# Modulation matrix multiplied as plain float32 on four 32-column tiles, with straight-line programs

## The chip, the cores and the metric

One core of one Trainium2 chip. The metric is device time of the whole kernel in microseconds; the kernel before takes 3344.34 us (median of three runs). PE is the engine for matrix products (TensorE), DVE VectorE, ACT ScalarE, POOL GpSimd, SP SyncE; SP and POOL only issue transfers here.

## What is computed

One inference step of a two-layer backbone on 128 context and 128 latent tokens of width 2048, all in float32. Layer 0 mixes tokens by attention, layer 1 by a two-directional state-space scan; each is followed by an MLP of width 8192. Every sub-layer is modulated, from a linear map of a conditioning vector:

```python
def ada_mod(cond, w, b):
    m = jax.nn.silu(cond) @ w + b          # w: 2048 x 12288 for each layer
    return jnp.split(m[:, None, :], 6, axis=-1)

for i in range(DEPTH):                     # 2 layers
    mp = ada_mod(c_ctx[None, :], mod_w[i], mod_b[i])   # context tokens
    ms = ada_mod(c, mod_w[i], mod_b[i])                # latent tokens
    hp = modulate(rms_norm(xp, norm_mix[i]), mp[0], mp[1])   # h * (1 + scale) + shift
    ...                                    # attention or scan
    xp = xp + mp[2] * op
    hp = modulate(rms_norm(xp, norm_mlp[i]), mp[3], mp[4])
    xp = xp + mp[5] * (jnp.square(jax.nn.relu(hp @ mlp_w1[i])) @ mlp_w2[i])
    ...                                    # the same for xs with ms
```

So the modulation matrices (two of 2048 x 12288, 201 MB) meet only two vectors, silu(c_ctx) and silu(c), while the other weights (some 450 MB) meet 256 tokens.

## The kernel before

All weights stream through SBUF in chunks of 1 MB (512 x 512 float32, as four blocks of 128 rows side by side, 2 KB pieces). A chunk lands in one of four slots of `raw`, in the order that SP issues. Each chunk is **split**: ACT writes `w_hi`, the rounding of `raw` to the reduced float32r type (two halves of 128 x 1024), and DVE writes `w_lo` = `raw` - `w_hi` (`split`, lines 441 and 697; two buffers of each). A slot is free again when DVE has read it (`lo_ready`).

An **L chunk** is one of a weight matrix. PE multiplies 16 blocks of 128 x 128: `hi` with 512 columns (256 tokens, high and low part; line 1111) and `lo` with the 256 high columns (lines 1110 and 1113), into four PSUM banks. Four L chunks (2,048 rows) make a **group** of 512 outputs; then ACT evacuates the right half of each bank (line 490), DVE adds the left half (line 787) and does the group's own work (`finish`).

An **M chunk** is one of the modulation matrix, split in the same way. PE holds as weights a window of `cond_w` (four columns carry silu of both vectors, high and low, the rest is other blocks' columns or zeros) and streams 512 columns of `w_hi` and then `w_lo` for each of four row blocks: eight products (line 1094) into bank `MROW`. After four M chunks ACT copies four rows of `MROW` to `m_rows` (line 478), four small float32 products with `comb` turn them into columns in `MCOL` (line 1141), and DVE adds the bias into `modv` (line 767): 48 times in all.

`layout` lists the phases. A phase has a pattern: "M" (eight groups of M chunks first, the shift and scale of layer 0), "LM" (an M chunk ahead of each L chunk: q, k, v, wo, the four `up0` and z) and "L" (the rest). There are 192 M and 432 whole L chunks. On each engine the middle groups of a phase are a hardware loop (`runs`, `Fori`), the first and last are written out.

Each engine's program is in order. At the end of a group ACT and DVE split the next chunk first (`nxt`) and evacuate then; in an LM phase that next chunk is an M chunk, so the first L chunk of the next group is split after the evacuation. Norms (`norm`) run between phases: ACT squares, 16 float32 products with ones on PE (line 1158), root, reciprocal, and then per quarter of the rows scaling on DVE and the high and low operand; some splits stand between these steps by `first_splits`. The scan of layer 1 is straight-line code; there, products on two 64-column tiles of the array alternate (`unit`, line 1318), beside products on the whole array (lines 1328 and 1347).

Of the kernel before, what the change touches and what calls it, by code (L numbers as in the profile page):

```python
# [25 lines left out]
ALU = mybir.AluOpType  # L26
# [22 lines left out]
HALF = CH_KT // 2 * CH_N  # L49
RAW_SLOTS = 4  # L50
MOD_BLOCKS = 6 * KT
N_QUARTERS = DFF // D

PAT = {
    "M": [("M", q) for q in range(4)],
    "L": [("L", q) for q in range(4)],
    "LM": [(t, q) for q in range(4) for t in ("M", "L")],
}


class Phase:


    def __init__(self, name, kind, pat, n, w=None, k0=0, c0=0, mod=None, operand=None, width=CH_N, **more):
        self.name, self.kind, self.pat, self.n = name, kind, pat, n
        self.w, self.k0, self.c0, self.mod, self.operand, self.width = w, k0, c0, mod, operand, width
        self.more = more
        self.chunks = PAT[pat]
        self.m = len(self.chunks)


def layout(ins):

    (mod_w, w1, w2, wqkv, wo, w_in, w_out) = (ins[k] for k in (
        "mod_w", "mlp_w1", "mlp_w2", "na_wqkv", "na_wo", "ssm_w_in", "ssm_w_out"))
    ph = [Phase("mod", "mod", "M", 8, mod=(0, 0))]
    for j, kind in enumerate("qkv"):
        ph.append(Phase(kind, kind, "LM", 4, w=wqkv[0], c0=j * D, mod=(0, 8 + 4 * j), operand="HL"))
    ph.append(Phase("wo", "res", "LM", 4, w=wo[0], mod=(0, 20), operand="HID", layer=0, gate=2 * KT))
    for layer in range(2):  # L80
        if layer == 1:
            ph.append(Phase("dt", "dt", "L", 1, w=w_in[0], c0=D_INNER + XBC_TILES * P, operand="HL", width=P))
            ph.append(Phase("z", "z", "LM", 8, w=w_in[0], c0=0, mod=(1, 16), operand="HL"))
            ph.append(Phase("xbc", "xbc", "L", 12, w=w_in[0], c0=D_INNER, operand="HL"))
            for half in range(2):
                ph.append(Phase(f"wout{half}", "res", "L", 4, w=w_out[0], k0=half * KT,
                                operand=("HL", "HID")[half], layer=1, gate=2 * KT))
        for quarter in range(N_QUARTERS):
            ph.append(Phase(f"up{layer}_{quarter}", "w1", "L" if layer else "LM", 4, w=w1[layer], c0=quarter * D,
                            mod=None if layer else (1, 4 * quarter), operand="HL"))  # L90
            ph.append(Phase(f"down{layer}_{quarter}", "res", "L", 4, w=w2[layer], k0=quarter * KT,
                            operand="HID", layer=layer, gate=5 * KT))
    t = g = mg = 0
    for p in ph:
        p.T0, p.G0, p.M0 = t, g, mg
        t += p.m * p.n
        g += p.n if "L" in p.pat else 0
        mg += p.n if "M" in p.pat else 0
    return ph


def chunk_source(ins, p, col0, typ, q):

    if typ == "M":
        layer, g0 = p.mod
        view = ins["mod_w"][layer].rearrange("(t p) n -> p t n", p=P)
        return view[:, 4 * q:4 * q + 4, bass.ds(g0 * CH_N + col0, CH_N)]
    view = p.w.rearrange("(t p) n -> p t n", p=P)
    return view[:, p.k0 + 4 * q:p.k0 + 4 * q + 4, bass.ds(p.c0 + col0, p.width)]


def program(nc, ins, outs):
    ph = layout(ins)
    by_name = {p.name: p for p in ph}
    N_CHUNKS = ph[-1].T0 + ph[-1].m * ph[-1].n
    owner = [p for p in ph for _ in range(p.m * p.n)]

    def by_block(p, c):


        typ, q = p.chunks[c]
        return typ == "L" and (q == 3 or (q == 0 and p.pat == "L") or p.width < CH_N)

    def read_count(T, u):

        p = owner[T]
        return 4 * T + 4 if by_block(p, (T - p.T0) % p.m) else 4 * T + 2 * (u + 1)

    ctx = ExitStack()
    with ctx:  # L130
# [48 lines left out]
        comb = sb("comb", [4, 2])  # L179
# [6 lines left out]
        csil = sb("csil", [P, 2, KT], offset=at_R + 40960)  # L186
# [37 lines left out]
        w_read = sem("w_read")  # L224
        evac = sem("evac")
        bank_free = sem("bank_free")
        group_out = sem("group_out")
        e2_step = sem("e2_step")
# [36 lines left out]
        G_END = {p.name: p.G0 + p.n for p in ph if "L" in p.pat}  # L265
        block = ctx.enter_context(nc.Block())

        def runs(eng, p, body):

            if p.n <= 2:  # L270
                for i in range(p.n):
                    body(i, 0)
                return
            body(0, 0)
            if p.n == 3:
                body(1, 0)
            else:
                with eng.Fori(0, p.n - 2) as s:
                    body(1, s)
            body(p.n - 1, 0)  # L280

        def first_splits(p):


            if p.pat == "LM":
                return {0: ((), (2,)), 1: ((), (3, 4)), 2: ((), (5, 6)), 3: ((), (7,))}
            return {0: ((), ()), 1: ((), ()), 2: ((2,), ()), 3: ((3,), ())}

        after_norm = {1, 5, 13, 16, 18}


        @block.sync
        def _(sp):
# [28 lines left out]
            for p in ph:  # L322
# [1100 lines left out]
```

## Time and profile before

| | |
|---|---|
| timed runs | 3344.34 us median, 3342.19 to 3346.95 |
| profiled execution, span first to last instruction | 3336.6 us |
| median of the runs above that span | 7.7 us |
| PE, DVE, ACT busy | 94%, 66%, 52% of the span |
| transfers | 696.17 MB, 209 GB/s mean over the span |

The profiled execution is one execution; the page gives its span, and its own time is that span with what lies around it, for which the only figure is the distance to the timed runs. In the rows, `bank<-HL,w_hi` means that the instruction writes `bank` and reads `HL` and `w_hi`; L1111 is a line of the kernel; `x192` counts records. A float32 product leaves two weight-load and two matmul records (a high and a low half), a float32r product one of each. PEclk is the granted TensorE clock as a share of full speed. Records of PE overlap in its pipeline.

### The profile page before, as it was taken

What the parts mean: (1) busy time and instruction counts of PE and PEld (TensorE: products, weight loads), DVE (VectorE), ACT (ScalarE), POOL (GpSimd) and SP (SyncE); (2) the same over time, 40 slices, a digit from 0 to 9 for tenths busy, and PEclk for the clock granted to TensorE, in tenths of its full rate; (3) what the DMA queues carried; (4) which work ended last, traced back from release to release, by engine and by line L of the source; (5) the groups of instructions that cost most, each with busy time, mean ns of one, the idle gap of its engine ahead of it and who ended that gap; (6) DMA issues with size and microseconds to landing.
All of it is one profiled execution on the core that took longest, in us unless ns stands there. A gap on an engine that the chain in (4) does not pass through costs nothing.

```text
span 3336.6 us, 47767 instructions
## 1 busy us (share of the span) xinstructions
PE 3119.8 (94%) x17357; PEld 2663.5 (80%) x17357; DVE 2215.8 (66%) x2980; ACT 1723.2 (52%) x2247; POOL 44.2 (1%) x71
## 2 busy tenths in 40 slices
PE   6899998989999999999699999966698999999998
PEld 4688887878888888888588888856587888888887
DVE  7866666777666676675666566777766665666565
ACT  5655555555455454454466555567443444444443
POOL 1000000000000000000000000011000000000000
PEclk9999999999999999999899999977899999999999
DMA  9777774757567576674477655556254555555552
GB/s 321 267 273 262 272 274 151 263 197 271 189 239 252 182 271 214 218 273 151 162 253 252 241 176 189 188 171 192 81 188 151 169 184 189 189 179 186 190 188 88
DMA packets 378477, 696.17 MB, mean 209 GB/s; under 512 B 12192, under 2 KB 55392, under 8 KB 377360
## 3 DMA queue, kind: packets, MB, share of 16 engines
q1 hardware_dynamic: 373568, 676.38, 59.3%
q0 software_dynamic: 4816, 18.69, 1.6%
q8 instruction: 42, 0.69, 0.1%
q14 instruction: 51, 0.42, 0.0%
HBM read 686.50 MB, written 8.52 MB: 208 GB/s over the span
## 4 chain that ended last, share of the span: by engine, by line
PE 39%; DVE 7%; issue 2%; ACT 2%; DMA 1%; SPq 1%; DVEq 0%; ACTq 0%; POOL 0%; POOLq 0%
PE bank L1111 24%; PE bank L1110 12%; PE bank L1094 1%; DMA bc_prompt<-ac_scratch 1%; DVE w_lo L697 1%; ACT w_hi L441 1%; PE bank L1113 1%; SPq L311 1%; DVE bc_prompt L992 0%; PE bank L1359 0%; DVE ROOM L746 0%; DVE xd L958 0%; DVE ROOM L751 0%; DVE ROOM L757 0%; DVE bc_prompt L948 0%
## 5 line engine op out<-in xcount | busy, mean ns | idle before, releaser
L697 DVE TENSOR_TENSOR w_lo<-raw,w_hi 128x1024 fp32r<-128x1024 f32 x1256 | 1481.1, 1217 | 731.3 <-ACT w_hi L441 730.9
L441 ACT ACTIVATE w_hi<-raw 128x1024 fp32r<-128x1024 f32 x1256 | 1268.0, 1050 | 1028.3 <-PE bank L1111 999.2
L1111 PE MATMUL bank<-HL,w_hi 128*128 128x512 f32 x4368 | 1549.7, 401 | 68.8 <-DVE HL L815 28.6
L1110 PE MATMUL bank<-HL,w_lo 128*128 128x256 f32 x4095 | 1162.8, 284 | 27.6 <-DVE HL L815 13.7
L1111 PEld LDWEIGHTS bank<-HL,w_hi 128*128 128x128 f32 x4368 | 814.4, 190 | 252.4 <-issue 61.3
L1111 PE MATMUL bank<-HID,w_hi 128*128 128x512 f32 x2560 | 894.2, 398 | 0.3 <-DVE w_lo L697 0.3
L1110 PEld LDWEIGHTS bank<-HL,w_lo 128*128 128x128 f32 x4095 | 781.1, 191 | 63.8 <-DVE w_lo L697 28.9
L1110 PE MATMUL bank<-HID,w_lo 128*128 128x256 f32 x2400 | 674.8, 281 | 0.0
L1111 PEld LDWEIGHTS bank<-HID,w_hi 128*128 128x128 f32 x2560 | 471.1, 188 | 105.1 <-issue 1.5
L1110 PEld LDWEIGHTS bank<-HID,w_lo 128*128 128x128 f32 x2400 | 453.6, 189 | 7.7 <-DVE w_lo L697 0.7
L787 DVE TENSOR_TENSOR U<-bank,U 128x256 f32<-128x256 f32 x433 | 181.1, 422 | 257.5 <-ACT U L490 257.4
L490 ACT ACTIVATE U<-bank 128x256 f32<-128x256 f32 x433 | 164.0, 383 | 339.6 <-PE bank L1111 336.4
L1094 PE MATMUL bank<-w_hi,cond_w 128*128 128x512 f32 x768 | 312.9, 407 | 8.3 <-DVE w_lo L697 7.3
L1094 PE MATMUL bank<-w_lo,cond_w 128*128 128x512 f32 x768 | 305.2, 397 | 0.0
L1094 PEld LDWEIGHTS bank<-w_hi,cond_w 128*128 128x128 f32 x768 | 146.1, 190 | 45.0 <-DVE w_lo L697 16.8
L1094 PEld LDWEIGHTS bank<-w_lo,cond_w 128*128 128x128 f32 x768 | 146.0, 190 | 31.2
L738 DVE SCALAR_TENSOR_TENSOR X<-U,modv,X 128x128 f32<-128x128 f32 (+1 forms) x352 | 96.1, 345 | 0.4
L1113 PE MATMUL bank<-HL,w_lo 128*128 128x256 f32 x273 | 79.2, 290 | 0.0
L1113 PEld LDWEIGHTS bank<-HL,w_lo 128*128 128x128 f32 x273 | 55.0, 202 | 11.4
L1141 PEld LDWEIGHTS bank<-comb,m_rows 4*128 4x128 f32 x384 | 46.2, 186 | 19.3 <-issue 9.9
L515 ACT ACTIVATE HL<-SQ 128x1024 fp32r<-128x1024 f32 x16 | 16.9, 1058 | 81.7 <-DVE SQ L833 81.7
L1141 PE MATMUL bank<-comb,m_rows 4*128 4x2 f32 x384 | 50.3, 249 | 5.9 <-ACT m_rows L478 5.9
(203 smaller groups left out, 1377.0 us busy)
## 6 DMA issues: line engine op xcount, KB each, us to landing
raw<-in_mlp_w SPq DMA_DIRECT2D x256, 1024.0 KB, 5.2
raw<-in_mod_w SPq DMA_DIRECT2D x192, 1024.0 KB, 6.0
raw<-in_ssm_w_in SPq DMA_DIRECT2D x80, 1024.0 KB, 5.0
raw<-in_na_wqkv SPq DMA_DIRECT2D x48, 1024.0 KB, 5.1
raw<-in_ssm_w_out SPq DMA_DIRECT2D x32, 1024.0 KB, 5.0
raw<-in_na_wo SPq DMA_DIRECT2D x16, 1024.0 KB, 5.0
bc_prompt<-ac_scratch SPq DMA_DIRECT2D x16, 512.0 KB, 5.7
bc_sample<-ac_scratch SPq DMA_DIRECT2D x16, 512.0 KB, 6.0
```

The lines of the kernel that those rows point to most:

```text
L311: sp.dma_start(ea[64 * h:64 * h + 64, d, :, :], src).then_inc(ea_in, 16)
L441: nc.scalar.activation(w_hi[:, T % 2, u * n:(u + 1) * n], raw[:, T % RAW_SLOTS, u * n:(u + 1) * n], ACT.Copy).then_inc(hi_ready, 1)
L490: i = nc.scalar.activation(U[:, b, :], bank[b][:, TOK:2 * TOK], ACT.Copy)
L515: nc.scalar.activation(HL[:, 4 * t:4 * t + 4, 0:TOK], SQ[:, 4 * t:4 * t + 4, :], ACT.Copy).then_inc(oper_hi, 1)
L697: nc.vector.tensor_tensor(w_lo[:, T % 2, s], raw[:, T % RAW_SLOTS, s], w_hi[:, T % 2, s], ALU.subtract).then_inc(lo_ready, 1)
L738: i = nc.vector.scalar_tensor_tensor(xt, U[:, b, r * SEQ:(r + 1) * SEQ], gt, xt, ALU.mult, ALU.add)
L787: i = nc.vector.tensor_tensor(U[:, b, :], bank[b][:, 0:TOK], U[:, b, :], ALU.add)
L1094: i = nc.tensor.matmul(MROW[:, :], lhs, w[:, slot, kt * CH_N:(kt + 1) * CH_N], start=first, stop=last)
L1110: nc.tensor.matmul(bank[b][:, 0:TOK], lo, a[:, 0:TOK], start=False, stop=False)
L1111: i = nc.tensor.matmul(bank[b][:, :], hi, a, start=first, stop=last)
L1113: i = nc.tensor.matmul(bank[b][:, 0:TOK], lo, a[:, 0:TOK], start=False, stop=False)
L1141: i = nc.tensor.matmul(MCOL[:, 2 * b:2 * b + 2], m_rows[:, b * P:(b + 1) * P], comb[:, :], start=True, stop=True)
```

## The change

The M chunk becomes 128 rows of 2,048 columns (8 KB pieces), read by PE directly from `raw` as plain float32. The weights are 32 columns (`cond`: silu of the two vectors and 30 zeros), and four products per chunk go to four 32-column tiles of the array, so that tile j writes partitions 32j to 32j + 31 of `MROW`. A block of 2,048 outputs takes 16 M chunks; then ACT copies all of `MROW` once, four products with `pick` turn it, and DVE adds the bias for 16 tiles of 128: 12 times in all. M chunks are no longer split; their slot is freed by PE (`m_read`). The load order is a list: 32 M chunks first, then one ahead of each L chunk of the former LM phases. All loops are written out. All groups now follow the order of the former L phases: the next L chunk's split stands ahead of the evacuation, and the by-block order of products holds at the first and last chunk of each group. The first norm moves into the first M stage. Core of the diff:

```diff
+def load_order(ph):
+    order = [("M", m) for m in range(MOD_FIRST)]
+    m = MOD_FIRST
+    for p in ph:
+        for i in range(4 * p.n):
+            if p.mod:
+                order.append(("M", m))
+                m += 1
+            order.append(("L", p.T0 + i))
+    return order
...
+def mod_source(ins, m):
+    layer, block, kt = m // (6 * KT), m // KT % 6, m % KT
+    return ins["mod_w"][layer][kt * P:(kt + 1) * P, block * D:(block + 1) * D]
...
-        cond_w = sb("cond_w", [P, KT * 4 + P - 4], F32R)
-        cond = cond_w[:, 0:KT * 4].rearrange("p (t v) -> p t v", v=4)
+        cond = sb("cond", [P, KT, 32])
-        m_rows = sb("m_rows", [4, CH_N])
+        m_rows = sb("m_rows", [P, CH_N])
...
# SP
+            for at, (typ, n) in enumerate(order):
+                if at >= RAW_SLOTS:
+                    gone, g = order[at - RAW_SLOTS]
+                    if gone == "L":
+                        sp.wait_ge(lo_ready, 2 * (g + 1))
+                    else:
+                        sp.wait_ge(m_read, g + 1)
...
# ACT
+            def mod_rows(block):
+                act.wait_ge(m_read, KT * (block + 1))
+                if block:
+                    act.wait_ge(m_cols, block)
+                nc.scalar.activation(m_rows[:, :], MROW[:, :], ACT.Copy).then_inc(m_rows_in, 1)
...
+                    if T + 4 < N_CHUNKS:
+                        split(T + 4)
+                    block = block_done(T)
+                    if block is not None:
+                        mod_rows(block)
...
+            squares(range(4))
+            norm_root()
+            for block in range(2):
+                mod_rows(block)
+            split(0)
+            split(1)
+            operand(by_name["q"])
...
# DVE, first norm
+                if k == 0:
+                    dve.wait_ge(rms_root, 1)
+                    link(nc.vector.reciprocal(rbc[:, :], rbc[:, :]))
+                    mod_bias(0)
+                    mod_bias(1)
+                    split(0)
                 if not last:
...
+                    split(p.T0 + 1)
...
# PE
-                                    for part, w in enumerate((w_hi, w_lo)):
-                                        i = nc.tensor.matmul(MROW[:, :], lhs, w[:, slot, kt * CH_N:(kt + 1) * CH_N],
-                                                             start=first, stop=last)
+            def mod_chunk(m):
+                block, kt = m // KT, m % KT
+                slot, full = loaded("M", m)
+                pe.wait_ge(raw_in[slot], full)
+                if kt == 0 and block:
+                    pe.wait_ge(m_rows_in, block)
+                for j in range(4):
+                    i = nc.tensor.matmul(MROW[32 * j:32 * j + 32, :], cond[:, kt, :],
+                                         raw[:, slot, j * CH_N:(j + 1) * CH_N], start=kt == 0, stop=kt == KT - 1)
+                i.then_inc(m_read, 1)
+            def mod_cols(block):
+                pe.wait_ge(m_rows_in, block + 1)
+                if block:
+                    pe.wait_ge(mod_out, block)
+                for b in range(4):
+                    i = nc.tensor.matmul(MCOL[:, 8 * b:8 * b + 8], m_rows[:, b * P:(b + 1) * P], pick[:, :],
+                                         start=True, stop=True)
+                i.then_inc(m_cols, 1)
...
+            for m in range(MOD_FIRST):
+                mod_chunk(m)
+                if m == KT // 2:
+                    norm()
+                if m % KT == KT - 1:
+                    mod_cols(m // KT)
```

In a phase, PE calls `mod_chunk` ahead of the L chunk that it stands before in the list, and `mod_cols` after the first L chunk of the group that follows a finished block.

## Rows read from the trace of the kernel before

**Rows 1.** The page: busy times; costly groups (count, busy us, mean ns, idle); a transfer.

```profile
PE 3119.8 (94%) x17357; PEld 2663.5 (80%) x17357; DVE 2215.8 (66%) x2980; ACT 1723.2 (52%) x2247; POOL 44.2 (1%) x71
...
L697 DVE TENSOR_TENSOR w_lo<-raw,w_hi 128x1024 fp32r<-128x1024 f32 x1256 | 1481.1, 1217 | 731.3 <-ACT w_hi L441 730.9
L441 ACT ACTIVATE w_hi<-raw 128x1024 fp32r<-128x1024 f32 x1256 | 1268.0, 1050 | 1028.3 <-PE bank L1111 999.2
...
raw<-in_mod_w SPq DMA_DIRECT2D x192, 1024.0 KB, 6.0
```

**Rows 2.** Windows: M and L chunks; L alone; first M stage (busy, clock, DMA).

```profile
391.59:484.98 93.39, 93.39 (x505) 79.38 (x505) 62.76 (x65) 53.71 (x64) 0.00 (x0) 1.00 0.76 270
2765.59:2856.00 90.41, 90.41 (x514) 78.56 (x513) 55.95 (x65) 38.86 (x48) 0.00 (x0) 1.00 0.56 186
39.00:106.00 67.00, 60.25 (x254) 42.33 (x253) 58.65 (x56) 53.10 (x57) 0.00 (x0) 0.99 1.04 383
```

**Rows 3.** Windows of line 1111 alone: stretch, us, PE, PEld, clock, DMA share, GB/s.

```profile
391.59:484.98 93.39, 67.37 (x192) 35.47 (x193) 1.00 0.76 270
2765.59:2856.00 90.41, 89.28 (x258) 47.05 (x256) 1.00 0.56 186
134.68:173.49 38.81, 24.08 (x64) 12.72 (x65) 0.94 0.54 190
...
707.26:1589.69 882.43, 722.07 (x2048) 379.40 (x2048) 0.99 0.65 224
2576.87:2607.51 30.64, 25.84 (x65) 13.90 (x65) 0.84 0.31 103
1636.37:1892.81 256.44, 181.55 (x512) 95.12 (x512) 0.99 0.74 258
1898.10:2173.44 275.34, 268.53 (x768) 141.49 (x768) 1.00 0.53 180
```

**Rows 4.** The chain that ended last, in z: start, us, what.

```profile
1709.34 1.86 PE bank L1094 x8
```

**Rows 5.** Timelines of PE, wide and narrow windows: start, us, engine, line, records.

```profile
690.75 1.05 PE L1141 MATMUL bank<-comb,m_rows 4*128 4x2 f32 x8
691.73 7.17 PE L1158 MATMUL bank<-SQ,one 128*128 128x256 f32 x32
...
2216.68 1.95 PE L1347 MATMUL bank<-ROOM,h0T 128*128 128x128 f32 x16
2218.56 1.97 PE L1318 MATMUL bank<-bc_sample,xd 128*64 128x128 f32 x32
...
2218.36 0.28 PE L1347 MATMUL bank<-ROOM,h0T 128*128 128x128 f32 x1
2218.56 0.33 PE L1318 MATMUL bank<-bc_sample,xd 128*64 128x128 f32 x2
...
2218.56 0.44 PE L1318 MATMUL bank<-bc_sample,xd 128*64 128x128 f32 x4
...
2327.66 0.28 PE L1318 MATMUL bank<-bc_prompt,xd 128*64 128x128 f32 x2
2327.86 0.38 PE L1328 MATMUL bank<-rbc,xd 128*128 128x128 f32 x1
```

**Rows 6.** Timeline at the end of down0_0 and before z.

```profile
930.58 3.89 ACT L441 ACTIVATE w_hi<-raw 128x1024 fp32r<-128x1024 f32 x4
...
934.63 0.79 PE L1111 MATMUL bank<-HL,w_hi 128*128 128x512 f32 x1 [2.53 <-DVE w_lo L697]
...
1636.37 0.79 PE L1111 MATMUL bank<-HL,w_hi 128*128 128x512 f32 x1 [7.39 <-DVE w_lo L697]
```

**Rows 7.** DMA queues from 2196 to 2330 us: packets, MB, share of 16 engines.

```profile
q8 instruction: 6, 0.10, 0.3%
```

**Rows 8.** Timeline of the start, PE.

```profile
26.91 0.48 PE L1094 MATMUL bank<-w_hi,cond_w 128*128 128x512 f32 x1
...
134.68 0.79 PE L1111 MATMUL bank<-HL,w_hi 128*128 128x512 f32 x1 [5.51 <-DVE HL L815]
```

More of the change, by code:

```diff
@@ L48 @@
 CH_N = 512
-HALF = CH_KT // 2 * CH_N
 RAW_SLOTS = 4
 MOD_BLOCKS = 6 * KT
+MOD_CHUNKS = 12 * KT
+MOD_FIRST = 2 * KT
 N_QUARTERS = DFF // D
[L54 to L58, printed above, removed]
-class Phase:
[L64 to L69, printed above, removed]
@@ L114, in program, with loaded, mods_before, block_done @@
     by_name = {p.name: p for p in ph}
[L115 to L122, printed above, removed]
+    N_CHUNKS = ph[-1].T0 + 4 * ph[-1].n
+    owner = [p for p in ph for _ in range(4 * p.n)]
+    order = load_order(ph)
+    place_of = {what: at for at, what in enumerate(order)}
+    def loaded(typ, n):
+        at = place_of[typ, n]
+        return at % RAW_SLOTS, 16 * (at // RAW_SLOTS + 1)
+    def mods_before(T):
+        at = place_of["L", T]
+        start = place_of["L", T - 1] + 1 if T else MOD_FIRST
+        return [n for _, n in order[start:at]]
+    def block_done(T):
+        for t in range(T // 4 * 4, T // 4 * 4 + 4):
+            for m in mods_before(t):
+                if m % KT == KT - 1:
+                    return m // KT
+        return None
+    def by_block(T):
+        return T % 4 in (0, 3) or owner[T].width < CH_N
     def read_count(T, u):
-        p = owner[T]
-        return 4 * T + 4 if by_block(p, (T - p.T0) % p.m) else 4 * T + 2 * (u + 1)
+        return 4 * T + 4 if by_block(T) else 4 * T + 2 * (u + 1)
     ctx = ExitStack()
@@ L263, in program, with first_splits @@
         f_sc, f_t, f_sb, f_done = (sem(n) for n in ("f_sc", "f_t", "f_sb", "f_done"))
-        G_END = {p.name: p.G0 + p.n for p in ph if "L" in p.pat}
+        G_END = {p.name: p.G0 + p.n for p in ph}
         block = ctx.enter_context(nc.Block())
[L268 to L289, printed above, removed]
+        def first_splits(t):
+            return {2: (2,), 3: (3,)}.get(t, ())
+        after_norm = {"q", "up0_0", "dt", "wout0", "up1_0"}
         @block.sync
@@ L459, in silu @@
                     nc.scalar.activation(v, v, ACT.Silu).then_inc(silu_out, 1)
-                def body(rep, shift):
+                for rep in range(p.n):
                     last = rep == p.n - 1
-                    for c in range(1, p.m):
-                        if rep or k not in after_norm:
-                            split(p.T0 + rep * p.m + c, p.m, shift)
+                    gi, T = p.G0 + rep, p.T0 + 4 * rep
+                    if rep or name not in after_norm:
+                        for c in (1, 2, 3):
+                            split(T + c)
@@ L713, in finish, with phase @@
+            def phase(name):
+                p = by_name[name]
+                def finish(rep):
+                    dve.wait_ge(bank_free, 4 * (p.G0 + rep + 2))
+                    tiles = slice(4 * rep, 4 * rep + 4)
                     Uall = U[:, :, :]
-                    def step(i, s):
-                        i.then_inc(e2_step, 1)
-                        dve.wait_ge(e2_step, e2_0 + steps * rep + s + steps * shift)
                     if p.kind in "qkv":
@@ L796, in _, with norm @@
             norms = [0]
-            def norm(layer, scale, shift_, gain, p=None, last=False):
+            def norm(layer, scale, shift_, gain, p=None, blocks=0, last=False):
                 k = norms[0]
                 norms[0] += 1
+                if k == 0:
[4 more added lines that the diff above has]
+                    split(0)
                 if not last:
-                    dve.wait_ge(mod_out, 1 + max(p.M0 + p.n for p in ph if "M" in p.pat and p.T0 < cur[0]))
+                    dve.wait_ge(mod_out, blocks)
@@ L939, in _ @@
             dve.wait_ge(ac_w, 16)
-            phase(15)
+            phase("xbc")
             def segments(g):
@@ L1402, in constants @@
     c[:, 4] = np.where(ok[turned], 0.0, NEG)
-    c[[0, 1, 2, 3], 5, [0, 1, 0, 1]] = 1.0
+    for j in range(4):
+        c[[32 * j, 32 * j + 1], 5, [2 * j, 2 * j + 1]] = 1.0
     return c
```

513 lines of the change are left out of this document (211 added, 302 removed).

## The prediction

> **What bounds the kernel now.** I read the page first. TensorE (PE) is busy 94% of the span, VectorE 66%, ScalarE 52% [rows 1]. PE's records overlap in its pipeline, so their sums are no prices; starts and stretches are. Then the stages: in a stretch where a modulation ("M") chunk goes before every weight ("L") chunk, and in one with L chunks alone, PE is busy the whole time, DVE 67% and 62%, ACT 58% and 43%, the DMA engines 0.76 and 0.56 [rows 2]. So PE sets the pace of both. In the first M stage (39 to 106 us) the DMA engines are full at 383 GB/s, with PE at 90%: DMA sets that one.
>
> Next the pace, by line 1111 (16 records per L chunk, 64 per group of four). L alone: 90.41 us for four groups, 22.60 each. With M: 93.39 us for three groups, 31.13 each [rows 3]. The difference, 8.53 us, is four M chunks and one small transposing product: the latter's eight records take 1.05 us [rows 5], an M chunk (line 1094, eight records) 1.86 us [rows 4], and 4 x 1.87 + 1.05 = 8.53. So 1.87 us per M chunk is PE's real price.
>
> **The change, part by part.**
>
> *The new M chunk on PE.* It holds 128 rows by 2,048 columns, as many numbers as before: four float32 matmuls of 512 columns, each a high and a low record. Plain float32 is in the trace: 32 records of 256 columns take 7.17 us [rows 5], about 0.216 us a record, so a 512-column record is 0.433 us. Eight in turn would be 3.46 us, nearly twice today's 1.87. All depends on whether the column tiles run at once. The trace shows no four tiles of 32 columns, but two of 64, also in float32, in the scan. There 32 records of 128 columns take 1.97 us; on the whole array 16 records take 1.95 us [rows 5]: 0.055 against 0.11 us a record. The narrow windows say how: the records come in pairs, from the first on; one on the whole array lasts 0.28 us, the first two here together 0.33 and the first four 0.44, so each pair starts together, 0.11 after the pair before. So two tiles do run side by side, each with its own high and low half in turn. If four do the same, the chunk is two steps of 0.433 = 0.87 us.
>
> Bounds: 0.87 us below; 3.46 us above (in turn); and 4 x 0.433 = 1.73 us if no more than the two streams that the trace shows are fed at once. I take 0.87, because the pairs show tiles as independent and nothing in the rows as a limit of two.
>
> *Changing the tile shape.* From whole array to 64 columns the next start comes 0.20 us after the last instead of 0.11, and the first record is 0.33 us long, not 0.28; going back it is 0.20 instead of 0.11, and 0.38, not 0.28 [rows 5]. That is 0.14 + 0.19 = 0.33 us a visit; each M chunk between L chunks is a visit. So 0.87 + 0.33 = 1.20 us, 0.67 less than now; bounds 0.87 (changes hidden) to 3.8.
>
> A rule speaks against the four at once. The pairs above start with the very first records. The Trainium skill (TensorE: Matmul & The Clock Gate, Part 3, "What overlaps and what doesn't") says that matmuls start and end strictly in order, and that a weight load overlaps a running matmul only in another row group, while column tiles share all rows. By that a tile's low half waits for its high half, and the next tile queues behind it: five steps. The trace disagrees for two tiles; no run here shows four. The rule's time is a rival below.
>
> *Transposing product.* Once per 16 chunks instead of four: 0.26 us a group instead of 1.05. A group with M is then 22.60 + 4 x 1.20 + 0.26 = 27.66 us.
>
> *ACT and DVE.* 384 splits of 1.05 and 1.22 us [rows 1] leave. Neither sets the pace, so by itself this is worth nothing; it pays where an L chunk's split stood late. At the end of an L phase that an M phase follows, ACT splits the next L chunk only after the last evacuation (930.58), DVE after its residual operations, and PE waits 2.53 us for it (934.63) [rows 6]. Now the split of the next L chunk stands ahead of the evacuation, as in L phases, where groups keep 22.6 us. The same order holds at every group of z.
>
> *Transfers.* A pair of chunks (2.1 MB) in 27.66 / 4 = 6.9 us is 304 GB/s; 383 has been granted [rows 2], so it is hidden. If only today's 270 came, the pair would take 7.8 us and all the gain of these stages would be lost. An M slot is now freed by PE, and SP's next L load queues behind that wait. With M done 1.2 us into a pair, the M load takes 6.0 us [rows 1] and the L load behind it 2.7 more: landed at 9.9, first half split at 12.2 (1.05 + 1.22). PE wants it at 13.8 + 1.2 = 15.0, so 2.8 us spare.
>
> *Straight-line programs.* A loop's return costs PE nothing now: in L phases 64 pairs of 0.353 us make the whole 22.60. So no gain there. More instructions must be fetched. In the scan, straight-line already, 6 packets came on PE's instruction queue in 134 us [rows 7], one per 22 us. I take zero, because PE's products in that stage run on at 0.11 and 0.055 us a record [rows 5]; exposed, a packet is about 1.1 us (0.3% of 16 engines' 134 us, over 6).
>
> *The start.* PE's first M chunk stands at 26.9 us, behind the transposes of x, and the first L product at 134.7 [rows 8]. Between 27 and 39 us slots still wait for M splits behind bias work on DVE; now PE frees them directly. From about 29 us DMA is full: 32 more chunks (M4 to M33, L0, L1; DVE splits L1 ahead of the first scaling) at 1.05 MB / 383 GB/s = 2.74 us, plus 3.3 us of latency (6.0 - 2.7), end at 120. Split of L1 3.3 (two halves on ACT, one more on DVE), then scaling, shift, copy and low half, an estimate of 5.7 (five passes of 128 x 1024 at 1.05 to 1.22): first L product at 129 us, now 134.7, so 6 us. The norm's 7.2 us on PE moves under the loads; the wait for L1 eats most of that. Bounds: nothing, or 22 us if the loads come faster.
>
> *Sum* [rows 3, 6]:
> - start: 6
> - q to wo: 15 groups x (31.13 - 27.66) = 52; the first, 38.81, becomes about 31, like the first group after a norm without M (30.64): 8
> - layer 0's MLP, 882.43 us: 31 + 15 x 27.66 + 16 x 22.60 = 807.5, and 1 from M0 under the norm: 76
> - z, 256.44 us: 8 x 27.66 = 221.3: 35. After dt, PE waits 7.39 us for z's first L split, held behind ACT's dt work; that split now comes first and its 5.65 us of products and an M chunk fill the wait: 7
> - xbc, 275.34 us against 12 x 22.60 = 271.2: 4, less 1 for the last transposing product: 3
>
> Together 187 us: 3336.6 - 187 = 3149.6 of span. The shown median is 7.7 us above the profiled span; I keep that: **3157 us**.
>
> **Rivals.**
> 1. *Four tiles at once* (forecast): 3157. For it the pairs; against it that only two are seen.
> 2. *Two streams at a time*: 1.73 + 0.33 = 2.06 us a chunk, 0.86 x 160 = 138 us back: 3295. For it: two float32 streams (512 columns in 0.433 us each) take columns about as fast as today's float32r stream (512 in 1.86 / 8 = 0.233), and no row shows more.
> 3. *In turn*, slower than before: if a tile's low half waits for its high half and the next tile's records queue behind it in order, five steps of 0.433 + 0.33 = 2.50 us a chunk give 208 back, 3365; wholly in turn 3.8 us, 416 back, and the 28 first chunks PE-bound at 3.8 instead of 2.74 (30 us): about 3603. It decides from 1.20 + 187 / 160 = 2.37 us a chunk. Against it the pairs in rows 5. The skill's order rule, above, is the five steps.
> 4. *Fetches exposed*: one packet per 22 us as in the scan, 143 x 1.1 = 157 us: 3314. Against it: the even pace of the scan's products.
> 5. *More gain*: shape changes hidden behind the last L product (160 x 0.33 = 53) and a quicker start (15): about 3090.
>
> **How the numbers follow.** Chances: 0.55 for the first, 0.20 for the second, 0.11 for the third, 0.06 for the fourth, 0.08 for the fifth. The time is the first's, 3157; its own range is 3120 to 3190 (0.1 us of shape change is 16 us, the start 15). For 8 in 10 the range reaches from the near half of the fifth to the second: 3105 to 3303. Faster by over 0.2% (what a measurement of this kernel can tell from no change): the first, second, fifth and half of the fourth, 0.86; same, the other half of the fourth (packets dearer still), 0.03; slower, the third, 0.11.
>
> **What would show it.** In the changed profile: records of the M products on 32 columns starting in fours 0.43 us apart, an M chunk about 1.2 us from the L product before to the one after; groups with M at 27.7 us and without at 22.6; near 300 GB/s in those stages with PE still busy throughout; transposing products 12 times, not 48; no ACT splits of M; no PE wait at L-to-M phase changes; first L product near 129 us. Steps of twos (1.7 us a chunk) mean rival 2, single ones rival 3. Wrong otherwise, if PE waits for raw data in the M stages, or waits of no cause come at even distances of instructions (fetches).

## The result and the profile after

The changed kernel takes 3134.91 us (median of four runs, 3133.77 to 3138.26) where the kernel before took 3344.78 in the same comparison: a ratio of 0.9379, interval 0.9365 to 0.9392. The forecast was 3157 (3105 to 3303), so the time lies 22 us below it and inside the range. The profiled span is 3133.4 us against 3336.6.

The page of the changed kernel, busy times and groups as in [rows 1]:

```profile
PE 2921.3 (93%) x17069; PEld 2371.7 (76%) x17069; DVE 1763.6 (56%) x2559; ACT 1279.7 (41%) x1796; POOL 44.0 (1%) x71
...
q8 instruction: 135, 2.21, 0.3%
...
L694 DVE TENSOR_TENSOR w_lo<-raw,w_hi 128x1024 fp32r<-128x1024 f32 x872 | 1033.9, 1216 | 941.7 <-ACT w_hi L439 941.7
L439 ACT ACTIVATE w_hi<-raw 128x1024 fp32r<-128x1024 f32 x872 | 884.6, 1049 | 1221.5 <-PE bank L1089 614.7
...
L1055 PE MATMUL bank<-raw,cond 128*32 128x512 f32 x1536 | 217.8, 644 | 25.6 <-DMA raw<-in_mod_w 25.6
```

L1055 is the new M product, L1089, L1091 and L1088 are the L products, L694 and L439 the splits on DVE and ACT. The 384 splits of M on each of these engines are gone (1256 to 872), and that takes 447 us of work from DVE and 383 from ACT; PE, whose records overlap, gives up 198. PE stays busy for 93% of the shorter span.

The stages, as windows of all engines (columns as in [rows 2]): three groups with M, four of L alone, the first M stage, z, xbc, layer 0's MLP.

```profile
264.95:346.19 81.24, 81.24 (x485) 60.52 (x481) 34.60 (x41) 28.69 (x37) 0.00 (x0) 1.00 0.85 306
2562.43:2652.84 90.41, 90.41 (x514) 78.52 (x513) 56.01 (x65) 38.75 (x48) 0.00 (x0) 1.00 0.60 188
39.00:106.00 67.00, 46.77 (x236) 12.98 (x240) 1.95 (x2) 1.07 (x2) 0.00 (x0) 0.70 0.94 387
...
1474.20:1691.47 217.27, 216.98 (x1285) 162.84 (x1282) 95.31 (x111) 87.11 (x111) 0.00 (x0) 1.00 0.85 307
1696.42:1968.16 271.74, 271.74 (x1547) 236.22 (x1545) 184.06 (x278) 129.58 (x158) 0.55 (x1) 1.00 0.54 183
635.97:1435.22 799.25, 798.27 (x4641) 642.28 (x4642) 444.56 (x584) 308.69 (x391) 0.00 (x0) 1.00 0.71 248
```

Against [rows 3], L alone has not moved: 90.41 us for four groups then and now. Three groups with M went from 93.39 to 81.24, so one is 27.08 us. An M chunk is then (27.08 - 22.60) / 4 = 1.12 us where it was 1.87; it was forecast at 1.20. PE is still busy without a gap in these stages, and DMA carries 306 GB/s there (forecast 304), so the transfers stayed hidden. The first M stage is still set by DMA (387 GB/s); PE is busy there for 47 of 67 us only.

One M chunk between two L chunks in PE's timeline, then the same chunk in narrow windows (start, us, engine, line, records):

```profile
433.72 0.39 PE L1089 MATMUL bank<-HL,w_hi 128*128 128x512 f32 x1
434.04 1.07 PE L1055 MATMUL bank<-raw,cond 128*32 128x512 f32 x8
435.04 0.39 PE L1088 MATMUL bank<-HL,w_lo 128*128 128x256 f32 x1
435.26 0.40 PE L1089 MATMUL bank<-HL,w_hi 128*128 128x512 f32 x1
...
434.04 0.62 PE L1055 MATMUL bank<-raw,cond 128*32 128x512 f32 x2
...
434.04 0.64 PE L1055 MATMUL bank<-raw,cond 128*32 128x512 f32 x4
...
434.49 0.61 PE L1055 MATMUL bank<-raw,cond 128*32 128x512 f32 x4
...
434.04 0.16 PEld L1055 LDWEIGHTS bank<-raw,cond 128*32 128x32 f32 x8 [0.25 <-issue]
```

The first two records together last 0.62 us and the first four 0.64: four products on four tiles start within about 20 ns. The second four start at 434.49, 0.45 us behind the first. So a chunk is two steps of 0.45 us, as the forecast had it (0.433). The five steps that were worked out for the third rival from the order rule in the Trainium skill (TensorE: Matmul & The Clock Gate, Part 3, "What overlaps and what doesn't") do not happen: no tile's high half waits for another's low half. The weight loads do not keep to that rule either, by which one overlaps a running product only in another row group: all eight of the chunk are over at 434.20 us, while its first products, on the same 128 rows, run until 434.66. The same part of that page, under "Measured speedup vs the span model", gives a measured speedup of 2.38 times for three column tiles; here four tiles make an M chunk 3.35 / 1.12 = 3.0 times as fast as the whole array does (first experiment, changes of shape included), which is in line with it.

The start, with the releaser in brackets:

```profile
116.23 2.00 ACT L439 ACTIVATE w_hi<-raw 128x1024 fp32r<-128x1024 f32 x2 [3.21 <-DMA raw<-in_na_wqkv]
117.39 2.36 DVE L694 TENSOR_TENSOR w_lo<-raw,w_hi 128x1024 fp32r<-128x1024 f32 x2 [2.82 <-ACT w_hi L439]
119.67 2.18 DVE L818 SCALAR_TENSOR_TENSOR SQ<-X,modA,rbc 128x128 f32<-128x128 f32 x8
...
125.52 0.80 PE L1089 MATMUL bank<-HL,w_hi 128*128 128x512 f32 x1 [13.28 <-DVE HL L805]
```

L1 lands at 116.2, its split on DVE ends at 119.7, and the first quarter of the operand follows: the first L product stands at 125.5 where it stood at 134.7 [rows 8]; the forecast was 129, with L1 landed at 120.

### The profile page after: what moved, and what is told of

The parts are those of the page before. It is cut to its first block, busy times and chain, and to the rows that moved or that the text cites. A ratio compares the mean times of both kernels' runs of the same rounds, so it can differ in the third digit from the quotient of the medians.

```text
span 3133.4 us, 40784 instructions
## 1 busy us (share of the span) xinstructions
PE 2921.3 (93%) x17069; PEld 2371.7 (76%) x17069; DVE 1763.6 (56%) x2559; ACT 1279.7 (41%) x1796; POOL 44.0 (1%) x71
## 4 chain that ended last, share of the span: by engine, by line
PE 44%; DVE 5%; DMA 1%; ACT 1%; issue 1%; SPq 1%; POOL 0%; DVEq 0%; ACTq 0%; POOLq 0%
PE bank L1089 28%; PE bank L1088 13%; DMA bc_prompt<-ac_scratch 1%; PE bank L1055 1%; PE bank L1091 1%; SPq L313 1%; PE bank L1327 1%; DVE w_lo L694 0%; DVE bc_prompt L969 0%; DVE xd L935 0%; DVE ROOM L1028 0%; DVE bc_prompt L925 0%; DVE ROOM L1026 0%; DVE SQ L818 0%; DVE ROOM L944 0%
## 5 line engine op out<-in xcount | busy, mean ns | idle before, releaser
L1089 PE MATMUL bank<-HL,w_hi 128*128 128x512 f32 x4368 | 1542.2, 399 | 56.2 <-DVE HL L805 38.0
L694 DVE TENSOR_TENSOR w_lo<-raw,w_hi 128x1024 fp32r<-128x1024 f32 x872 | 1033.9, 1216 | 941.7 <-ACT w_hi L439 941.7
L439 ACT ACTIVATE w_hi<-raw 128x1024 fp32r<-128x1024 f32 x872 | 884.6, 1049 | 1221.5 <-PE bank L1089 614.7
L1088 PE MATMUL bank<-HL,w_lo 128*128 128x256 f32 x4095 | 1167.7, 285 | 18.6 <-DVE HL L805 16.9
L1089 PEld LDWEIGHTS bank<-HL,w_hi 128*128 128x128 f32 x4368 | 811.7, 189 | 256.9 <-DVE HL L805 41.5
L1089 PE MATMUL bank<-HID,w_hi 128*128 128x512 f32 x2560 | 892.0, 397 | 0.0
L1088 PEld LDWEIGHTS bank<-HL,w_lo 128*128 128x128 f32 x4095 | 780.1, 191 | 123.4 <-issue 89.2
L1088 PE MATMUL bank<-HID,w_lo 128*128 128x256 f32 x2400 | 675.9, 282 | 0.0
L1089 PEld LDWEIGHTS bank<-HID,w_hi 128*128 128x128 f32 x2560 | 470.8, 188 | 104.5 <-issue 2.5
L1088 PEld LDWEIGHTS bank<-HID,w_lo 128*128 128x128 f32 x2400 | 453.6, 189 | 16.8 <-issue 10.1
L1055 PE MATMUL bank<-raw,cond 128*32 128x512 f32 x1536 | 217.8, 644 | 25.6 <-DMA raw<-in_mod_w 25.6
L1055 PEld LDWEIGHTS bank<-raw,cond 128*32 128x32 f32 x1536 | 31.5, 110 | 98.9 <-DMA raw<-in_mod_w 56.5
L736 DVE SCALAR_TENSOR_TENSOR X<-U,modv,X 128x128 f32<-128x128 f32 x352 | 96.3, 348 | 0.4
L1091 PE MATMUL bank<-HL,w_lo 128*128 128x256 f32 x273 | 77.3, 283 | 0.0
L1091 PEld LDWEIGHTS bank<-HL,w_lo 128*128 128x128 f32 x273 | 53.0, 194 | 11.1
L1091 PE MATMUL bank<-HID,w_lo 128*128 128x256 f32 x160 | 44.5, 278 | 0.0
L728 DVE TENSOR_TENSOR HID<-U,HID 128x1024 fp32r<-128x1024 f32 x32 | 39.2, 1225 | 1.1
L1276 PE MATMUL bank<-ident,U 128*128 128x128 f32 x64 | 12.2, 354 | 29.1 <-DVE ea L998 23.7
L726 DVE SCALAR_TENSOR_TENSOR U<-U 128x1024 f32<-128x1024 f32 x32 | 39.1, 1221 | 0.3
```

The source lines that it names most:

```text
L439: nc.scalar.activation(w_hi[:, T % 2, u * n:(u + 1) * n], raw[:, slot, u * n:(u + 1) * n], ACT.Copy).then_inc(hi_ready, 1)
L694: nc.vector.tensor_tensor(w_lo[:, T % 2, h], raw[:, slot, h], w_hi[:, T % 2, h], ALU.subtract).then_inc(lo_ready, 1)
L726: link(nc.vector.scalar_tensor_tensor(Uall, Uall, 0.0, Uall, ALU.max, ALU.mult))
L728: i = nc.vector.tensor_tensor(HID[:, tiles, TOK:2 * TOK], Uall, HID[:, tiles, 0:TOK], ALU.subtract)
L736: i = nc.vector.scalar_tensor_tensor(xt, U[:, b, r * SEQ:(r + 1) * SEQ], gt, xt, ALU.mult, ALU.add)
L1055: i = nc.tensor.matmul(MROW[32 * j:32 * j + 32, :], cond[:, kt, :], raw[:, slot, j * CH_N:(j + 1) * CH_N], start=kt == 0, stop=kt == KT - 1)
```

## The experiments

**Does the gain need four tiles at once?** In the first run the four products of a chunk go to the whole array, one after the other:

```diff
-i = nc.tensor.matmul(MROW[32 * j:32 * j + 32, :], cond[:, kt, :], ..., start=kt == 0, stop=kt == KT - 1)
+at = 96 + 18 * kt - 32 * j
+i = nc.tensor.matmul(MROW[:, :], cond_all[:, at:at + P], ...,
+                     start=kt == 0 and j == 0, stop=kt == KT - 1 and j == 3)
```

> Only the place of the M products changes: the four float32 products of a chunk go to the whole array (128 columns, the vector of its 32-column tile in its place and zeros beside it) one after another, as the L products do; nothing else moves, and there is no change of tile shape. If the four tiles running at once are what pays: a chunk becomes eight records of 0.433 us in turn, 3.46 us instead of 1.12, so 160 x 2.34 = 374 us more between the L chunks, and the 28 first chunks become PE-bound at 3.46 instead of 2.74 us, 20 more: about 3530 us, slower than the kernel before. If plain float32 by itself (no split, no second stored half) were what pays, with the tiles of no account, it stays near 3135.

Measured: 3517.28 us, 1.0518 of the kernel before (1.0487 to 1.0548). Three groups with M take 108.04 us, 36.01 each, so an M chunk is (36.01 - 22.60) / 4 = 3.35 us:

```profile
341.46:449.50 108.04, 68.08 (x193) 35.36 (x193) 1.00 0.64 234
```

(the window of its L product alone, columns as in [rows 3]). Plain float32 without the tiles is slower than the kernel before, by 173 us.

In the second, two tiles of 64 columns take two products each, in the order 0, 2, 1, 3:

```diff
+for j in (0, 2, 1, 3):
+    at = 32 + 64 * kt - 32 * (j % 2)
+    i = nc.tensor.matmul(MROW[64 * (j // 2):64 * (j // 2) + 64, :], cond_all[:, at:at + 64], ...,
+                         start=kt == 0 and j % 2 == 0, stop=kt == KT - 1 and j % 2 == 1)
```

> The four products of a chunk go to two tiles of 64 columns, two products on each, issued to the two tiles alternately. By two streams side by side a chunk is four steps of about 0.44 us and the change of shape, some 2.0 us instead of 1.12: 160 x 0.88 = 141 us more, about 3275 (what the prediction's second rival described). If the width of a tile does not matter and the array takes all four anyway: 3135. If the two products on one tile also wait for each other's end, beyond 2.0 us a chunk: over 3290.

Measured: 3272.13 us, 0.9785 (0.9756 to 0.9813). Three groups with M take 91.62 us, 30.54 each, so a chunk is 1.99 us:

```profile
282.55:374.17 91.62, 67.17 (x192) 35.37 (x192) 1.00 0.76 275
...
326.20 0.39 PE L1092 MATMUL bank<-HL,w_hi 128*128 128x512 f32 x1
326.52 1.94 PE L1057 MATMUL bank<-raw,cond_all 128*64 128x512 f32 x8
328.39 0.39 PE L1091 MATMUL bank<-HL,w_lo 128*128 128x256 f32 x1
```

One, two and four tiles give 3.35, 1.99 and 1.12 us a chunk: each doubling about halves the products' part, and with more than one tile a part for the change of shape stays. Rival 2 was priced nearly right (3295; the run with two streams took 3272). Rival 3's upper end, wholly in turn with changes of shape, was 3603; this run has none, and took 3517.

**How much of the gain is PE's M chunk?** The third run gives the M chunk its old form on PE (eight float32r products of 512 columns on the whole array) and leaves the rest as in the changed kernel:

```diff
+for part in range(2):
+    i = nc.tensor.matmul(MROW[:, :], cond_all[:, at:at + P], cond_all[:, :],
+                         start=kt == 0 and j == 0 and part == 0, stop=kt == KT - 1 and j == 3 and part == 1)
```

> The M chunk gets the length that it had before (eight float32r products of 512 columns on the whole array, 1.87 us), with everything else as in the changed kernel; the products read a constant block instead of the loaded chunk, so the modulation values are not the reference's, while the chunk's load, its wait and its release stay. If the M chunk's length on PE explains the part of the gain that was put down to it: 160 x (1.87 - 1.12) = 120 us more, about 3255, and the remaining 90 us against the kernel before come from the start, the order of the splits and the rarer transposing product. If the removed splits on ACT and DVE or the larger loads were worth something by themselves beyond that, it stays well under 3255; if the gain is all PE's M chunk, it goes back to about 3330.

Measured: 3241.72 us, 0.9694 (0.9665 to 0.9722). The chunk came to 1.81 us (three groups in 89.51 us), so 160 x 0.69 = 110 us were due and 107 came back. About half of the 210 us is PE's M chunk. The other 102 are in the rest, where this run's trace has them: the start (first L product at 126.5, 8 us earlier than before), the transposing product (0.8 us in 10 groups in place of 1.05 in 40, so 34), dt to z (7), and the first groups, z and changes of phase (layer 0's MLP takes 841.4 us here against 882.43 [rows 3], and from z's first product to xbc's first it is 243.2 instead of 261.7; 14 of these 41 us and 7 of these 18 are the transposing products).

**What does the order of the splits carry?** The next run moves, on ACT and on DVE, the split of the next group's first L chunk behind the evacuation, in all phases:

```diff
-if T + 4 < N_CHUNKS:
-    split(T + 4)
 for b in range(p.width // P):
 ...
+if T + 4 < N_CHUNKS:
+    split(T + 4)
```

> The split of L chunk T+4, on ACT and on DVE, goes behind the evacuation of a group that ends at T, as in the kernel before in its M phases, and here in the phases of L alone too. If splitting ahead of the evacuation is part of the gain: at each group's end the next chunk's halves come one evacuation later, and PE waits some 1 to 3 us at a share of the 100 or so groups, so 3135 becomes 3190 to 3350, and the gain at dt to z (7.7 us) goes. If the splits are early enough either way, since PE is four chunks behind (22 us), it stays within 10 us of 3135 and the gain is PE's M chunk alone.

Measured: 3555.04 us, 1.0631 (1.06 to 1.0661), far beyond the 3350 that was expected at most. The group of L alone becomes 27.3 us instead of 22.6. A group's end in that trace:

```profile
2897.65 0.38 ACT L483 ACTIVATE U<-bank 128x256 f32<-128x256 f32 x1 [1.02 <-PE bank L1089]
2897.93 3.89 ACT L439 ACTIVATE w_hi<-raw 128x1024 fp32r<-128x1024 f32 x4
...
2899.01 4.63 DVE L694 TENSOR_TENSOR w_lo<-raw,w_hi 128x1024 fp32r<-128x1024 f32 x4 [0.52 <-ACT w_hi L439]
...
2900.38 0.47 PE L1089 MATMUL bank<-HL,w_hi 128*128 128x512 f32 x1 [2.77 <-DVE w_lo L694]
...
2901.40:2904.40 3.00, 3.00 (x11) 2.59 (x11) 3.00 (x3) 0.42 (x1) 0.00 (x0) 0.50 0.60 143
```

(The last line is a window of all engines, columns as in [rows 2].) ACT makes the split only after the last block is evacuated, DVE follows it, and PE waits 2.77 us for the first product and 0.4 us again for the halves behind it. Then the granted clock is 0.50, the lower of its two levels, for some 3 us, and a pair of L products takes 0.64 us instead of 0.353. That is where the 4.7 us of a group come from: 3.2 us of waiting and some 1.5 us of slow products. The estimate was too low because it took a single wait of 1 to 3 us, at a share of the groups, and left out the clock; nearly every group of L alone pays all of it. Its other branch took PE to be four chunks behind the splits; but the halves have two buffers, so a split waits for PE's last read of the chunk two before and can be one chunk ahead at most.

Since that run also disturbs the L phases, the next one keeps the late split only where an M chunk stands ahead of the L chunk, which is where the kernel before had it:

```diff
-if T + 4 < N_CHUNKS:
+if T + 4 < N_CHUNKS and not mods_before(T + 4):
     split(T + 4)
 ...
+if T + 4 < N_CHUNKS and mods_before(T + 4):
+    split(T + 4)
```

> As the run with all splits behind the evacuation, but only where an M chunk stands ahead of the L chunk (as in the kernel before); groups that an L chunk without M follows keep the order of the changed kernel. If the shorter M chunk no longer covers a late split: the groups with M take 29.2 to 30.8 us as in that run, instead of 27.1, and the time is about 3135 + 40 x 2.7 = 3243: half of the change's gain hangs on the order of the splits. If that run's loss in M phases came from disorder that its L phases left behind: within 20 us of 3135.

Measured: 3254.44 us, 0.9729 (0.9711 to 0.9747). The first chunk of a group behind an M chunk, and one such group as a window of the L product:

```profile
274.11 1.06 PE L1059 MATMUL bank<-raw,cond 128*32 128x512 f32 x8
...
276.95 0.47 PE L1093 MATMUL bank<-HL,w_hi 128*128 128x512 f32 x1 [1.77 <-DVE w_lo L696]
...
291.89:321.14 29.25, 22.42 (x65) 11.78 (x64) 1.00 0.80 288
1104.03:1134.83 30.80, 23.75 (x64) 12.36 (x65) 0.94 0.78 270
```

The M chunk of 1.06 us is over before the split is, and PE waits 1.77 us; groups with M take 29.25 to 30.8 us. The two lengths differ by the granted clock behind the wait: 1.00 over a group of 29.25 us, 0.94 over one of 30.80 (the second window). So 120 of the 210 us hang on the order of the splits, and part of that price is the clock's.

Was the late split hidden behind the M chunk when that was long? The last run has both, the old length of the M chunk and the late split:

> The two runs before put together: the M chunk at its old length (1.8 us, products of a constant block in place of the loaded chunk, so the modulation values are not the reference's), and the split of an L chunk that has an M chunk ahead of it behind the evacuation. Alone, the old length took 3242 us and the late split 3254. If the longer M chunk covers the late split, it stays at 3242 (within 10 us). If the late split costs the same 120 us whatever stands ahead of it: 3361. Between: PE's wait of 1.77 us at a group's start shrinks by the 0.7 us that the M chunk is longer, so some 40 x 1.1 to 40 x 2.3 us are left: 3285 to 3335.

Measured: 3305.35 us, 0.9876 (0.9848 to 0.9905). With the long chunk the late split costs 3305 - 3242 = 64 us, with the short one 3254 - 3135 = 120. So the long chunk covered about half of it, the middle one of the three expectations. Three groups with M, and the start of one:

```profile
286.54:380.58 94.04, 67.54 (x192) 35.37 (x193) 1.00 0.75 268
...
315.01 2.01 PE L1062 MATMUL bank<-cond_all 128*128 128x512 f32 x8
317.95 0.47 PE L1098 MATMUL bank<-HL,w_hi 128*128 128x512 f32 x1 [0.93 <-DVE w_lo L697]
```

PE still waits 0.93 us at the group's start. A group is 31.35 us, no shorter than before (31.13), although most have lost the transposing product: the wait stands where that was. In the kernel before, with the same late split, PE has no wait in q, k and v behind the first group (173.5 to 512 us): there the M chunk and the transposing product behind it together covered the split.

The four runs make a square: late split and long chunk 3305 us, late and short 3254, early and long 3242, early and short 3135. With the late split the short chunk is worth 51 us, with the early one 107; the early split is worth 64 us with the long chunk and 120 with the short one. The two together are 170 of the 210 us, and the price of each depends on the other. The remaining 39 are the start, dt to z, the first groups and the rest.

**Is the price of the tile shape one of each visit?** Three runs put two M chunks into a visit. The first has the order M M L L:

```diff
-    if p.mod:
-        order.append(("M", m))
-        m += 1
+    if p.mod and i % 2 == 0:
+        order += [("M", m), ("M", m + 1)]
+        m += 2
```

> Only the load order changes in the phases that hold M chunks: M M L L instead of M L M L, so PE goes to the 32-column tiles 80 times between L chunks instead of 160 times, with two chunks each time. If part of an M chunk's 1.12 us is a price of each visit (1.12 less two steps of 0.44, some 0.24 us): 80 x 0.24 = 19 us less, 3116. If the price is one of each chunk (the waits for raw data, the first load of each tile): no change, 3135. If L loads that now stand two in a row behind two M loads come too late for their splits: up to 2.7 us a pair, slower than 3135.

Measured: 3151.64 us, 0.9424 (0.9412 to 0.9437): slower than the changed kernel by 17 us. Groups that run without a wait are 26.66 us, 0.42 less than 27.08, so the two visits saved are worth 0.21 us each; but the changes of phase lose more. The change from k to v:

```profile
343.56 2.01 ACT L439 ACTIVATE w_hi<-raw 128x1024 fp32r<-128x1024 f32 x2 [9.03 <-DMA raw<-in_na_wqkv]
345.47 0.58 ACT L447 ACTIVATE m_rows<-bank 128x512 f32<-128x512 f32 x1
345.95 1.20 ACT L485 ACTIVATE U<-bank 128x256 f32<-128x256 f32 x4
...
346.19 1.92 PE L1055 MATMUL bank<-raw,cond 128*32 128x512 f32 x16 [1.87 <-ACT m_rows L447]
```

The L chunk lands late behind two M loads, ACT waits 9.0 us for it, and behind its split stand the copy of the modulation rows and the evacuation, for which PE waits. From the last product of v to the first of wo it is 60.8 us instead of 56.2.

The next run keeps M M L L and lets ACT copy the rows ahead of that split:

```diff
+block = block_done(T)
+if block is not None:
+    mod_rows(block)
 if T + 4 < N_CHUNKS:
     split(T + 4)
-block = block_done(T)
-if block is not None:
-    mod_rows(block)
```

> The order M M L L once more, and on ACT the copy of the modulation rows goes ahead of the split of the next group's first chunk, instead of behind it. If PE's wait of 1.9 us at the change from k to v (released by that copy) is the whole loss of the M M L L run: it goes at ten or so block ends, and 3151 becomes about 3130. If the evacuation behind the same late split is the larger part, it stays within 10 us of 3151.

Measured: 3143.27 us, 0.9398 (0.9385 to 0.941). The wait for the rows is gone, the median is 8 us lower (the two profiled spans, 3143.8 and 3141.5, differ by 2.3 only), and at the same place PE now waits for the evacuation:

```profile
346.62 0.47 PE L1089 MATMUL bank<-HL,w_hi 128*128 128x512 f32 x1 [0.98 <-DVE U L774]
```

The third moves the pair to the second and the fourth L chunk of a group (the line above with `i % 2` in place of `i % 2 == 0`), so that the late load is one inside the group:

> Two M chunks a visit, as in the run with M M L L, but the pair stands before the second and the fourth L chunk of a group instead of the first and the third. In that run the L load behind two M loads was the one whose split ACT makes ahead of the evacuation and of the modulation rows, so both came late at group ends. Here the late load belongs to the fourth chunk, inside the group. If the lost time was that: groups with M at 26.6 to 26.7 us instead of 27.08, no waits at the phase changes, about 19 us less than the changed kernel: 3116 (3110 to 3125). If two M loads in a row make L late wherever they stand: 3135 to 3155, as in that run.

Measured: 3120.89 us, 0.9339 (0.9326 to 0.9352), 14 us below the changed kernel (0.9379, 0.9365 to 0.9392) and the fastest version here; the two profiled spans, 3119.1 and 3133.4, differ by the same 14. Half of the groups with M are 26.38 us, and from k to v there is no gap at all. A visit with two chunks:

```profile
401.18 0.39 PE L1089 MATMUL bank<-HL,w_hi 128*128 128x512 f32 x1
401.50 1.92 PE L1055 MATMUL bank<-raw,cond 128*32 128x512 f32 x16
403.35 0.39 PE L1088 MATMUL bank<-HL,w_lo 128*128 128x256 f32 x1
```

Here the two visits saved are worth 0.35 us each. So the change of shape is paid by the visit: between 0.21 and 0.35 us, by which visits are dropped. The difference lies in the L products that have no M chunk among them: sixteen pairs (a chunk's worth) take 5.47 to 5.55 us here and 5.66 to 5.76 in the M M L L run; why is open. Those dropped here include the one ahead of a group's first product. Were all 40 groups shorter by 0.70 us, it would be 28 us, not 14. Some of what is missing is seen in the trace: seven of the 80 visits last 2.0 to 4.2 us instead of 1.85, and from the last product of v to the first of wo it is 59.2 us instead of 56.2. What holds those up was not followed.

**Does L1's split set the start?** On ACT and on DVE the split of L1 goes behind the first quarter of the first operand:

```diff
-split(1)
-operand(by_name["q"])
+operand(by_name["q"], (1,))
```

> Only the first norm changes: on ACT and DVE the split of L1 goes behind the first quarter of the first operand, instead of ahead of it. In the changed kernel the first quarter (scaling at 119.7, low half at 124.2, first L product at 125.5) stands behind DVE's half of L1's split (117.4 to 119.7). If that is what the first L product waits for, it comes up to 5 us earlier, near 120, and the time is about 3130. If L1's split is then late for the second chunk, or the loads set the start anyway, the products wait there instead: within 2 us of 3135.

Measured: 3135.59 us, 0.9376 (0.9363 to 0.9388): no change. In that trace:

```profile
121.04 0.80 PE L1091 MATMUL bank<-HL,w_hi 128*128 128x512 f32 x1 [8.21 <-DVE HL L805]
...
137.95 0.39 PE L1090 MATMUL bank<-HL,w_lo 128*128 128x256 f32 x1 [1.93 <-DVE HL L805]
```

The first L product comes 4.5 us earlier, and the first group takes 34.2 us instead of 30.3: PE waits for a later quarter of the operand, since the same splits, scalings and halves stand on DVE in another order. With M M L L as well:

> The load order M M L L and the first norm's order together. If both pay and are independent: 19 + 5 us less, about 3111; if the pairs make the L loads late: 3135 or more; if only the visit's price is real: 3116.

Measured: 3145.66 us, 0.9411 (0.9398 to 0.9424), which is the M M L L run less 6, with intervals that overlap; neither expectation of a gain held, and the one of 3135 or more did.

## Why the prediction was right, and by how much it was off

The mechanism was right, term by term (us; measured is the difference between the two traces):

| term | predicted | measured |
|---|---|---|
| start | 6 | 9.2 (134.68 to 125.52) |
| q to wo | 52 + 8 | 63.4 (8.5 in the first group, 41.2 up to v's end, 13.7 in wo) |
| layer 0's MLP | 76 | 83.2 (882.43 to 799.25) |
| z | 35 | 39.2 (256.44 to 217.27) |
| dt to z | 7 | 7.7 |
| xbc | 3 | 3.6 (275.34 to 271.74) |
| sum | 187 | 206.3 |

Between the stages, attention and the scan took some 3 us more, so the spans differ by 203.2.

- *The M chunk.* Two steps side by side: shown by the narrow windows, and by the runs with one tile and with two. The mis-sized term is the change of shape, 0.33 us from the scan's rows. The two steps measured 0.91 instead of 0.87, the whole chunk 1.12 instead of 1.20, so the change, with all that goes with it, is 0.21 a visit: one size was too small and the other too large. The timeline puts the visit itself nearer to 0.29 and the rest in L products that run closer behind an M chunk (last section), a thing that the prediction held at 22.60 us a group. Over 160 chunks the difference is 13 us.
- *The transposing product.* 0.79 us a time (a group that holds one is 27.87 against 27.08) instead of 1.05: 2.6 us over ten.
- *The start.* The first L product was forecast behind L1's split and it is; it came 3.5 us earlier, because L1 landed at 116.2 us instead of 120; from there it is 9.3 us, where 9.0 were forecast. That the wait for L1 eats the rest is only half the reason: without it, DVE's work for the later quarters takes its place.
- *ACT and DVE.* That the removed splits are by themselves worth nothing is not shown by a run that puts them back; but the terms above leave nothing for them. The prediction credited the order of the splits with the waits at the ends of phases (the 2.53 us of [rows 6] among them) and with what z's groups take above 31.13 us. The runs with the late split show that all groups with M hang on it: with the short M chunk 120 us are lost, with the old length 64. The M work was a cover for the split, and the change shortens it; the prediction relied on the new order there without pricing it. In z, a table load made the late split late (last section), so there the right number had a second cause that the prediction did not see.
- *Transfers, fetches.* 306 GB/s against 304, and no wait of PE for raw data once the first M stage is over. The instruction queue's packets are 135 now, where rival 4 counted 143, and the groups of L alone kept 22.6 us to the hundredth, so rival 4 falls.
- *The offset.* 7.7 us were added from span to median, from the kernel before; the changed one needs 1.5. In every run whose own span is on record the time lies 1.7 to 2.9 us above the span of that same execution, before the change and after. So most of the 7.7 did not lie around the span: the profiled execution of the kernel before was 5 to 6 us faster than the median. That is 6 of the 22 us. The other 16 are the terms above.

## What to carry to other kernels

Where only a few columns of the weights are used, products on separate column tiles can run side by side; the price to put beside the halved steps is that of each change of tile shape, so fewer and longer visits pay where the loads still come in time. When an operation on the bounding engine is shortened, ask what it covered: here it and the transposing product were the cover of a split, and had the split not moved ahead of the evacuation, more than half of the gain would have been lost. And place the transfer that comes last where nothing of the group's end stands behind it on the same engine: the same pairs were 17 us slower or 14 us faster by one chunk's shift.

## What was not expected of the hardware

- ACT's table loads. The splits and silu in the former loops loaded a table 32 times in z and xbc, 1.28 us each; the written-out program does it twice. The lines of table loads of ACT from z to xbc, before and after, and the end of one of z's groups before:

```profile
L441 ACT ACT_TABLE_LOAD x16 | 20.5, 1283 | 0.7
L459 ACT ACT_TABLE_LOAD x16 | 20.5, 1283 | 0.3
```

```profile
L463 ACT ACT_TABLE_LOAD x2 | 2.6, 1283 | 0.0
```

```profile
1699.76 1.28 ACT L441 ACT_TABLE_LOAD   x1
1701.06 3.91 ACT L441 ACTIVATE w_hi<-raw 128x1024 fp32r<-128x1024 f32 x4
...
1703.51 0.49 PE L1111 MATMUL bank<-HL,w_hi 128*128 128x512 f32 x1 [1.16 <-DVE w_lo L697]
```

In z the load stood ahead of the late split, and PE waited for that split: 6.9 us in six waits, and groups of 32.5 us. In q, k and v, with the same order and no load, there was no such wait. In the run with the late split and the long M chunk, whose program is written out, z's groups take 31.4 us, as in the other phases with M. In xbc PE has no wait for a split, before or after. What the new order and the written-out program each gave in z, no run separates.

- The granted clock fell to a mean of 0.70 in the first M stage, where PE now waits for loads and is busy 47 of 67 us (0.99 before [rows 2]): part of the stage ran at the lower level, 1.2 GHz instead of 2.4. It cost nothing there, because DMA sets that stage: at 43.22 us a chunk lasts 1.93 us, behind a wait of 1.92 us for its load. In the runs with the late split, where PE sets the pace, the same fall behind a wait cost some 1.5 us a time.
- The change of shape is paid on both sides, as the scan's rows had it for 64 columns. The product before an M chunk keeps PE 0.32 us instead of 0.23 to the next start; the second step takes 0.55 us to the next L product instead of 0.45; and that product, 0.39 us long instead of 0.28, keeps PE 0.22 us instead of 0.12. Read so, a visit inside a group costs some 0.29 us, and the chunk with it 1.19 us, nearly the forecast 1.20. The mean over a group is lower, 1.12, because the L products behind an M chunk run closer: 0.346 us a pair (eleven pairs from 435.97 to 439.78 us) instead of 0.353. Why they do is not shown.
